# Entering the feed-forward: one half of x turned on VectorE in blocks through DRAM instead of on TensorE

## The reference, cut to what matters

```
x = x + rmsnorm(mixer(rmsnorm(x, g_pre_mix)), g_post_mix)
h = rmsnorm(x, g_pre_ffn)
f = (silu(h @ w_gate) * (h @ w_up)) @ w_down          # 1024 -> 2816 -> 1024
x = x + rmsnorm(f, g_post_ffn)                         # second block: 0.5 * rmsnorm(...)
```

## Time and profile before

| | us |
|---|---|
| median of 3 runs (lowest to highest) | 1746.89 (1746.23 to 1747.65) |
| the profiled execution | 1747.1 |
| its span | 1745.4 |
| TensorE busy in the span | 1732.7 (99%) |
| weight loads of TensorE busy (overlap it) | 1439.1 (82%) |
| VectorE busy | 1214.5 (70%) |
| ScalarE busy | 910.9 (52%) |
| GpSimd busy | 107.9 (6%) |

### The profile page before, as it was taken

The page is one execution under the profiler, slowest core; times in us unless marked ns, Lnnn a source line. Parts: engine busy times, 40 slices in busy tenths (PEclk is TensorE's granted clock), DMA queues, the critical chain, the costliest instruction groups (busy, mean ns, idle before and its releaser), DMA issues.

```text
span 1745.4 us, 22092 instructions
## 1 busy us (share of the span) xinstructions
PE 1732.7 (99%) x8189; PEld 1439.1 (82%) x8189; DVE 1214.5 (70%) x1583; ACT 910.9 (52%) x1390; POOL 107.9 (6%) x257
## 2 busy tenths in 40 slices
PE   8999999999999999999999999999999999999998
PEld 7888888888888888888888888888888888888887
DVE  8877656888666766566976766676656698676665
ACT  6664445666444544455564544454445556454443
POOL 5110000301000100001000100010000100010000
PEclk9999999999999999999999999999999999999999
DMA  8447776654877677868776587767786768657773
GB/s 269 153 145 234 226 228 207 186 181 140 243 226 227 194 241 242 255 200 266 235 251 193 174 247 227 222 198 235 239 256 210 258 219 262 201 172 234 226 223 122
DMA packets 335451, 378.16 MB, mean 217 GB/s; under 512 B 89744, under 2 KB 267440, under 8 KB 335088
## 3 DMA queue, kind: packets, MB, share of 16 engines
q1 hardware_dynamic: 332864, 369.00, 68.2%
q0 software_dynamic: 2176, 7.75, 1.4%
q10 hardware_dynamic: 304, 0.01, 0.0%
HBM read 350.48 MB, written 26.21 MB: 216 GB/s over the span
## 4 chain that ended last, share of the span: by engine, by line
PE 91%; DVE 4%; DMA 2%; ACT 1%; POOL 1%; issue 1%; SPq 0%; DVEq 0%; POOLq 0%; ACTq 0%
PE Dp L2119 17%; PE Dp L2121 17%; PE Dp L2120 17%; PE Gp L2121 6%; PE Tp L2121 6%; PE Tp L2120 6%; PE Gp L2120 6%; PE Gp L2119 6%; PE Tp L2119 6%; DVE wlo L1390 2%; DMA held_piece<-dil_masks 1%; PE Gp L2332 1%; DMA held_piece<-inner 1%; PE Tp L2134 0%; PE Gp L2134 0%
## 5 line engine op out<-in xcount | busy, mean ns | idle before, releaser
L1390 DVE TENSOR_TENSOR wlo<-raw,whi 128x1024 fp32r<-128x1024 f32 (+1 forms) x608 | 712.1, 1208 | 293.4 <-ACT whi L900 293.1
L900 ACT ACTIVATE whi<-raw 128x1024 fp32r<-128x1024 f32 (+1 forms) x608 | 607.6, 1046 | 424.9 <-PE Dp L2121 228.8
L2119 PE MATMUL Dp<-whi,a_hi 128*128 128x512 f32 (+2 forms) x764 | 289.7, 379 | 2.7 <-DVE wlo L1390 2.2
L2121 PE MATMUL Dp<-whi,a_lo 128*128 128x512 f32 (+2 forms) x764 | 285.6, 374 | 0.0
L2120 PE MATMUL Dp<-wlo,a_hi 128*128 128x512 f32 (+2 forms) x764 | 285.5, 374 | 0.0
L2119 PE MATMUL Dp<-whi,b_hi 128*128 128x512 f32 (+1 forms) x492 | 194.5, 395 | 0.0
L2121 PE MATMUL Dp<-whi,b_lo 128*128 128x512 f32 (+1 forms) x492 | 191.4, 389 | 0.0
L2120 PE MATMUL Dp<-wlo,b_hi 128*128 128x512 f32 (+1 forms) x492 | 191.3, 389 | 0.0
L2120 PE MATMUL Gp<-wlo,a_hi 128*128 128x512 f32 x480 | 186.8, 389 | 0.0
L2119 PE MATMUL Gp<-whi,a_hi 128*128 128x512 f32 x480 | 186.8, 389 | 0.0
L2121 PE MATMUL Tp<-whi,a_lo 128*128 128x512 f32 x480 | 186.8, 389 | 0.0
(11 more groups left out here) (271 smaller groups left out, 2027.7 us busy)
## 6 DMA issues: line engine op xcount, KB each, us to landing
raw<-in_ffn_w_gate_up SPq DMA_DIRECT2D x176, 512.0 KB, 5.0
raw<-in_w_in SPq DMA_DIRECT2D x132, 512.0 KB, 4.9
raw<-in_ffn_w_down SPq DMA_DIRECT2D x88, 512.0 KB, 4.4
raw<-in_w_gate SPq DMA_DIRECT2D x44, 512.0 KB, 4.1
raw<-in_w_up SPq DMA_DIRECT2D x44, 512.0 KB, 5.2
raw<-in_w_down SPq DMA_DIRECT2D x44, 512.0 KB, 4.5
held<-Z SPq DMA_DIRECT2D x132, 128.0 KB, 3.1
Z<-held SPq DMA_DIRECT2D x132, 128.0 KB, 4.8
```

Of the source, the lines that this page charges most:

```text
L900: return nc.scalar.activation(whi[g % W][0:rows, c0:c0 + n], raw[g % R][0:rows, c0:c0 + n], ACT.Copy).then_inc(hi_done, 1)
L1390: return V.tensor_tensor(wlo[g % W][0:rows, c0:c0 + n], raw[g % R][0:rows, c0:c0 + n], whi[g % W][0:rows, c0:c0 + n].bitcast(F32), ALU.sub ...
L2119: mm(o, hi, wh, start=start, stop=False, skip_group_check=True)
L2121: return mm(o, lo, wh, start=False, stop=stop, skip_group_check=True)
```

## The change

For the six feed-forward stages (`MOVED_X`), half c = 1 of x is no longer turned on TensorE. DVE turns x[:, t, 512:1024] in 32x32 blocks into `x_blocks(t)` (`turn_x`, one instruction for each tile), SP stores it to DRAM (`store_x`) and fetches it (`fetch_x`) into `stage[:, 1, :]`, the one buffer for both tiles. ACT multiplies the four 128-column groups by the norm gain in place (4 instructions) and rounds them into `a_hi` (1 instruction); DVE forms `a_lo` as before. The fetch of tile 1 waits until `a_lo` of tile 0's half is formed, since they share the buffer.

The first three pieces do their h = 0 units first: the new order is j0h0 j1h0 j2h0 j0h1 j1h1 j2h1 j3h0 down0 j3h1 down1 j4h0 j4h1 down2 and so on. The stores and fetches of the pieces' blocks move with them (`store_unit`), and the ACT and DVE work of pieces 0 to 3 moves to other steps. Some semaphores are merged (`iotas` and `ratios` into `con`, `cum_put` into `fg_dve`).

```diff
+MOVED_X = {s_ffn1(l) for l in range(LAYERS)} | HALVED
...
 def gu_unit(j, h):
-    return 2 * j + h if j < 3 else 3 * j - 2 - (j == NJ - 1) + h
+    if j < 3:
+        return 3 * h + j
+    return 6 + 2 * h if j == 3 else 3 * j - 2 - (j == NJ - 1) + h
...
 def dn_unit(j):
+    if j == 0:
+        return 7
     return 3 * j + 6 if j < NJ - 4 else NFFN - NJ + j
+
+
+def store_unit(j):
+    return 7 + 2 * j if j < 4 else gu_unit(j, 1) + 4
...
+            def store_x(t, s):
+                n = 2 * moves(s) + t
+                sp.wait_ge(x_turned, n + 1)
+                if n >= 2:
+                    sp.wait_ge(x_moved, 16 * (n - 1))
+                sp.dma_start(held_x[t], x_blocks(t)).then_inc(x_stored, 16)
+
+            def fetch_x(t, s):
+                sp.wait_ge(x_stored, 16 * (2 * moves(s) + t + 1))
+                if t == 1:
+                    sp.wait_ge(alo[0], 2 * s + 2)
+                else:
+                    sp.wait_ge(alo[1], 2 * s)
+                sp.dma_start(stage[:, 1, :].rearrange("p (q n) -> p q n", q=4),
+                             held_x[t].rearrange("(q c) (b n) -> (c b) q n", q=4, b=4)).then_inc(x_moved, 16)
...
                 for F in range(3 * LAYERS):
+                    u = g - ffn_base(F)
+                    if u == 3:
+                        store_x(0, ffn_stage(F))
+                        fetch_x(0, ffn_stage(F))
+                    elif u == 4:
+                        store_x(1, ffn_stage(F))
+                    elif u == 5:
+                        fetch_x(1, ffn_stage(F))
...
             def turned_hi(t, c, s):
+                if c == 1 and s in MOVED_X:
+                    act.wait_ge(x_moved, 16 * (2 * moves(s) + t + 1))
+                    for k in range(4):
+                        g0 = gain_col(s) + 4 + k
+                        ins = nc.scalar.activation(piece_cols(3)[:, k], piece_cols(3)[:, k], ACT.Copy, scale=prm[:, g0:g0 + 1])
+                    ins.then_inc(gn[t], 1)
                 act.wait_ge(gn[t], 2 * s + c + 1)
+                if c == 1 and s in MOVED_X:
+                    nc.scalar.activation(quad(a_hi, 1, t).rearrange("p k (q s) -> p k q s", q=4), piece_cols(3), ACT.Copy
+                                         ).then_inc(ahi[t], 1)
+                    return
...
                     turned_hi(1, 0, s + 1)
                     if last + W <= LAST:
                         hi_b(last + W)
-                    turned_hi(1, 1, s + 1)
+                    turned_hi(1 if s + 1 not in MOVED_X else 0, 1, s + 1)
                     first_eviction()
                     square_x(1, s + 1)
+                    if s + 1 in MOVED_X:
+                        turned_hi(1, 1, s + 1)
...
+            def turn_x(t, s):
+                dve.wait_ge(xr[t], 2 * s)
+                if moves(s):
+                    dve.wait_ge(x_stored, 16 * (2 * moves(s) + t - 1))
+                V.transpose(x_blocks(t).rearrange("p (b k c) -> p b k c", b=4, k=4),
+                            x[:, t, 512:1024].rearrange("p (k c b) -> p b k c", k=4, b=4)).then_inc(x_turned, 1)
...
                 residual(1, 1, s)
                 if s + 1 < STAGES:
+                    if moved_x:
+                        turn_x(1, s + 1)
                     lo(last - 1 + W, 0)
                     gained(1, 0, s + 1)
                     lo(last - 1 + W, 1)
-                    gained(1, 1, s + 1)
+                    if not moved_x:
+                        gained(1, 1, s + 1)
                     turned_lo(1, 0, s + 1)
-                    turned_lo(1, 1, s + 1)
+                    if not moved_x:
+                        turned_lo(1, 1, s + 1)
                     first_eviction()
                     refill(last)
+                    if moved_x:
+                        turned_lo(0, 1, s + 1)
+                        turned_lo(1, 1, s + 1)
...
             def turn_x_both(t, s):
                 turn_x(t, s, 0)
-                turn_x(t, s, 1)
+                if s not in MOVED_X:
+                    turn_x(t, s, 1)
...
                 def step(t, i, middle=None):
                     if i < 6:
-                        gate_up(t, i // 2, i % 2, middle)
+                        gate_up(t, i % 3, i // 3, middle)
+                    elif i in (6, 8):
+                        gate_up(t, 3, i // 2 - 3, middle)
+                    elif i == dn_unit(0):
+                        down(t, 0, middle)
```

More of the change, by code:

```diff
@@ L95, with turns, moves @@
 HALVED = {s_f21(l) for l in range(LAYERS)} | {s_f22(l) for l in range(LAYERS)}
+MOVED_X = {s_ffn1(l) for l in range(LAYERS)} | HALVED
+def turns(s):
+    return sum(1 if b in MOVED_X else 2 for b in range(s))
+def moves(s):
+    return sum(1 for b in MOVED_X if b < s)
 BY_CHUNK = {s_mix2(l) for l in range(LAYERS)}
@@ L654, in up @@
                         gate_up(g0 + gu_unit(j, h), wg, wu, l, h, FC * j, off + FC * j)
-                up(0)
-                up(1)
-                for j in range(2, NJ - 2):
+                for h in range(2):
+                    for j in range(3):
+                        gate_up(g0 + gu_unit(j, h), wg, wu, l, h, FC * j, off + FC * j)
+                gate_up(g0 + gu_unit(3, 0), wg, wu, l, 0, FC * 3, off + FC * 3)
+                two_rows(g0 + dn_unit(0), wd, l, 0)
+                gate_up(g0 + gu_unit(3, 1), wg, wu, l, 1, FC * 3, off + FC * 3)
+                two_rows(g0 + dn_unit(1), wd, l, 2)
+                for j in range(4, NJ - 2):
                     up(j)
@@ L973, in boundary @@
                     turned_hi(0, 0, s + 1)
-                    turned_hi(0, 1, s + 1)
+                    if s + 1 not in MOVED_X:
+                        turned_hi(0, 1, s + 1)
                     hi_a(last - 1 + W)
@@ L1016, in ffn_step @@
             def ffn_step(t, F, i, g0):
[L1017 to L1021, removed]
+                if i in (3, 4):
+                    gate_silu(t, F, i - 3, g0)
+                elif i in (5, 7, 9):
+                    f_hi_out(t, F, (i - 5) // 2, g0)
+                elif i in (6, 8):
+                    gate_silu(t, F, i // 2 - 1, g0)
+                elif i % 3 == 2 and 11 <= i <= 26:
                     f_hi_out(t, F, i // 3, g0)
@@ L1369, in _ @@
                 g0 = b + FFN1
-                boundary(s, g0 - 1, *hooks, lambda: ffn_step(0, f_1(l), 1, g0))
+                boundary(s, g0 - 1, *hooks, nothing)
                 swiglu(f_1(l), g0)
@@ L1380, in _ @@
                 g0 = mixer2(l) + 37
-                boundary(s_mix2(l), g0 - 1, nothing, nothing, lambda: ffn_step(0, f_22(l), 1, g0))
+                boundary(s_mix2(l), g0 - 1, nothing, nothing, nothing)
                 swiglu(f_22(l), g0)
-                end_of_ffn(s_f22(l), f_22(l), g0, lambda: ffn_step(0, f_21(l + 1), 1, base2(l + 1)))
+                end_of_ffn(s_f22(l), f_22(l), g0, nothing)
         @block.vector
@@ L1454, in turned_lo @@
                 dve.wait_ge(ahi[t], 2 * s + c + 1)
+                if c == 1 and s in MOVED_X:
+                    quarters = "p k (q s) -> p k q s"
+                    V.tensor_tensor(quad(a_lo, 1, t).rearrange(quarters, q=4), piece_cols(3),
+                                    quad(a_hi, 1, t).bitcast(F32).rearrange(quarters, q=4), ALU.subtract
+                                    ).then_inc(alo[t], 1)
+                    return
                 V.tensor_tensor(quad(a_lo, c, t), by4(stage[:, c, :]), quad(a_hi, c, t).bitcast(F32), ALU.subtract
@@ L1464, in boundary @@
                 after_residual()
+                moved_x = s + 1 in MOVED_X
                 if s + 1 < STAGES:
+                    if moved_x and between_gained is nothing:
+                        turn_x(0, s + 1)
                     gained(0, 0, s + 1)
                     between_gained()
-                    gained(0, 1, s + 1)
+                    if not moved_x:
+                        gained(0, 1, s + 1)
+                    elif between_gained is not nothing:
+                        turn_x(0, s + 1)
                 after_gained()
@@ L2098, in _ @@
                 hooks = mixing1(l)
-                boundary(s, g0 - 1, *hooks, lambda: ffn_step(0, f_1(l), 1))
+                boundary(s, g0 - 1, *hooks, nothing)
                 swiglu(f_1(l), g0)
@@ L2103, in _ @@
                 else:
[L2104 removed]
+                    end_of_ffn(s_ffn1(l), f_1(l), g0, nothing)
             for l in range(LAYERS):
@@ L2109, in _ @@
                 g0 = mixer2(l) + 37
-                boundary(s_mix2(l), g0 - 1, nothing, nothing, nothing, nothing, lambda: ffn_step(0, f_22(l), 1))
+                boundary(s_mix2(l), g0 - 1, nothing, nothing, nothing, nothing, nothing)
                 swiglu(f_22(l), g0)
-                end_of_ffn(s_f22(l), f_22(l), g0, lambda: ffn_step(0, f_21(l + 1), 1))
+                end_of_ffn(s_f22(l), f_22(l), g0, nothing)
         @block.tensor
@@ L2666 @@
     held_qk = [nc.dram_tensor(f"held_qk{i}", (P, 384), F32, kind="Internal").ap() for i in range(2)]
```

(3 more changed lines are left out.)

110 lines of the change are left out of this document (60 added, 50 removed).

## The result

The changed kernel takes 1757.56 us (median of 4 runs, 1756.00 to 1759.95) against 1746.99 for the kernel before in the same session: a ratio of 1.0059, 95% interval 1.0046 to 1.0071. It is slower, by 10.6 us where 4.2 were forecast, and the interval lies clear of 1. Its profiled execution has a span of 1756.8 us (time 1758.52), 11.4 more than before.

A forecast was written before the change was run, and what follows sets the result against it. TensorE's own work, busy 99%, was taken to bound the kernel. Minus 4.3 us of transposes plus 8.4 of waits gave +4.1 on 1747.1: 1751.2 us, own range 1748.5 to 1754.5, wide range 1744 to 1759.

The forecast's parts named there:

- The saving: TensorE at six feed-forward entries: two groups of four transposes fewer at each, 4.3 us in all, upper bound 5.2.
- VectorE's chain: Third entry: VectorE's queue from tile 1's residual to the end of tile 0's `a_lo`, 8.84 us, done at 612.83.
- What follows the landing: After tile 1's fetch: gain copies 1.26, `a_hi` 0.55, cast 1.05, half split 1.22, handings over 0.1 us.
- L = 3.0: Time for tile 1's 256 KB fetch to land, 3.0 us, bounds 2.2 and 4.8; each us counts 6 us.
- I am wrong if the fetch takes over 4: Sign against the forecast, at tile 1's fetch: over 4 us would point to its queueing behind unit 5's weights.
- The waits in all: TensorE's waits at step (0,4), unit 4's first, over six entries: 1.7 at two, 1.3 at two, 1.15 at two; 8.4 us.
- A wait of 0.1, which the later one contains: Third entry: unit 2's second half comes at 609.3, TensorE wants it at 609.2; contained in the wait at (0,4).
- For one of 1.3 I count no loss of clock.: TensorE's wait at (0,4): waits up to 0.7 left the clock at full speed, so 1.3 us was counted as costing none.
- Rival 1: At the entries the chain is hidden and only the transposes' time is left: 1742.8, faster; chance 0.14.
- Rival 2: Tile 1's fetch queues behind unit 5's weights and takes 4.8 us: 1762.0, slower; chance 0.13.
- Rival 3: The pieces' round trip is late, holding one split per feed-forward, 1 us each, adding 6: 1757; chance 0.12.
- Rival 4: Tile 1's fetch, little ahead of it, takes 2.2 us or nearly so: 1746.4 to 1748.5, no change; chance 0.11.

The follow-up runs named there:

- the early start: Changed kernel with tile 1's fetch into its own buffer: behind unit 5's weights 1751.11 us, issued ahead of them 1743.51 us.
- the three runs without the wait: Changed kernel with tile 1's half finished after units 4 and 5's splits, 1743.52 us; after unit 4's, 1743.97; or own buffer plus fetch ahead of weights, 1743.51.
- the order run: Changed kernel with both halves of x turned on TensorE again, only the new order of steps and pieces kept: 1746.76 us, ratio 1.0001.
- longer wait: Changed kernel plus one unused ScalarE copy of 1024 columns ahead of unit 4's split at each entry: 1765.82 us, ratio 1.0109.

## Why the prediction was right in its direction and short in its size

The measured 1757.56 lies inside the wide range of 1744 to 1759, but outside the forecast's own 1748.5 to 1754.5. The wait is where it was placed and for the reason given; its size is not.

**The saving** was 4.3 us, with bounds of 4.3 and 5.2; the two profiles give 4.5. Right.

**VectorE's chain.** Predicted 8.84 us from the residual of tile 1 to the end of tile 0's `a_lo`; in the trace 607.10 to 615.97, 8.87. The release of the fetch by `a_lo` followed within 0.1, as said. Right, and it was worked out wholly from durations of the kernel before.

**What follows the landing.** Gain copies 1.26, `a_hi` 0.55, cast 1.05, half split 1.22, 0.1 for handing over: 4.18. Measured from 619.89 to 624.12: 4.23. Right. I had named D as the bank of that wait; unit 4's first matmul writes G, which changes nothing in the sum.

**The fetch, L = 3.0**, is the term that was mis-sized. It took 2.99 to 4.89, mean 3.78; the six excesses add up to 4.65 us, close to half of the shortfall in the span. The bounds 2.2 and 4.8 nearly held it, and the sign "I am wrong if the fetch takes over 4" came true at one entry. I chose the single row of a fetch with the weights nearly landed over the median of those behind weights, as the weights had been issued 3.5 us before. The weights landed as I had worked out, the later of the two 2.6 us behind the fetch's start at the third entry and 1.8 to 2.2 at the others, where 1.8 was forecast. That weights right ahead count is shown for the early start, 4.7 against 3.0. For the start of the changed kernel it is 0.1 to 0.5 us; the rest of the excess over 3.0 varies from one execution to the next (4.89 to 3.09 at the fourth entry with the weights issued alike), and its source stays open. So part of the shortfall is the luck of the profiled execution.

**The waits in all.** Predicted standing for the six entries: 1.7, 1.7, 1.3, 1.15, 1.3, 1.15, 8.4 in all, (0,2) contained. Measured at (0,2) and (0,4) together: 1.78, 2.46, 2.49, 3.13, 1.86, 2.26, sum 14.0. With each entry's own L put in the place of 3.0 the prediction becomes 1.69, 2.37, 2.15, 3.04, 1.56, 2.14, sum 13.0, within 0.12 at four entries and 0.34 at the other two. So the differences between the entries, read from the lead of the residual over the transposes, were of the right kind, and most of the spread is L's.

**"A wait of 0.1, which the later one contains"**, for unit 2's second half. It measured 0.5 on average (3.0 in six). That it is contained is argued from the chain, which doesn't start from TensorE's steps: TensorE would have stood as much longer at (0,4). It fits that its removal brings 2.0 us where (0,4) has no wait. So it took nothing from the changed kernel but from any cure: it belongs to the price of the change once the wait is gone.

**"For one of 1.3 I count no loss of clock."** For waits of that size this held: none of 0.90 to 1.74 was followed by a fall. But the waits came out longer, and two of them (2.76 and 1.89) were, for 3.4 us in the profiled execution. Here the step failed that put the clock at nothing: the price of a wait beyond what the earlier trace rows show was left without an upper bound. (That the clock was at full speed in all 40 slices was also more than the earlier trace rows say; by windows it holds for the kernel before.)

**Sum.** 4.1 forecast, + 4.65 for L, + 3.4 for the clock, + 1.0 of standing that stays over, - 1.5 in the mixers, - 0.2 of more saving: 11.4, the measured difference of the spans.

**The rivals.** Rival 1 (hidden, 1742.8) didn't come about, but the three runs without the wait (1743.5, 1744.0, 1743.5) come within 1.2 us of it. In part that is chance: against the profile of before, these kernels still stand over 2 us in step (0,2), and have 1.4 us less in the mixers, for which no reason is known. Rival 2 (4.8 everywhere) held at one entry of six. Rival 3 has the number nearest to the measured one, 1757, but by chance: its mechanism (pieces late) is excluded by the order run at 1.0001, and by the list of waits, where no other group grew by more than 0.1 us. Rival 4 is excluded: no fetch of tile 1 landed in under 2.99 us in the changed kernel.

**What stays open** is what makes the clock fall behind one wait and not behind another, and whether work in the wait keeps it up; length alone doesn't tell. Also open is what sets the landing of a 256 KB fetch between 3.1 and 4.9 us in the same place of the order.

## What to carry to other kernels

When work moves from the bounding engine to a round trip through DRAM, count what is queued behind its consumer: here 0.36 us saved twice put 4 us of standing ahead of a split that TensorE needed within a step, and taking the fetched half one split later turned +0.6% into -0.2%. The landing time of such a transfer is a range and not a number: a place ahead of the weights made 1.7 us where these had been issued 1 to 2.5 us before, and 0.1 to 0.5 where it was 3.5, and if its wait ends on the path, it should be issued first or consumed late. A shared landing buffer hides as a start condition in the transfer's queue; an own buffer alone took the waits from 10.0 to 4.0 us, and only together with a place in the queue to none.

## What the hardware showed that I had not expected

The granted clock fell to the 1.2 GHz level for 3.41 us behind waits of 2.76 and 1.89 us (changed kernel) and of 3.24 and 1.91 (longer wait), and stayed at 2.4 GHz behind waits of 2.82, 2.60, 2.38 and 2.04 (longer wait) in the same place. Each fall cost 1.7 us, nearly as much as the shorter of these waits. By the mean clocks the number of falls varies between executions of one kernel; the changed kernel's spans lie 3.9 us apart, and the landing times that vary as well have a part in it that was not measured.
